# Hybrid layer step: convolution rows asked for by GpSimd, cache pages by SyncE, and one set of query weights for the last two routings

## The reference, cut to what matters

```python
xn = rmsnorm(hp, norm1[l])
qa, ka, va, qkv_b, z, b_raw, a_raw = project(xn, w_in[l], q_norm[l], k_norm[l])
oa = diff_attn_prompt(qa, ka, va, lam, slopes)               # group A, 4 heads
gq, gk, gv, gg, gbeta, conv_new = gdn_inputs(qkv_b, ...)      # group B: 4-tap convolution, silu
ob, s_new = gdn_prompt(gq, gk, gv, gg, gbeta)
hp = hp + merge_heads(oa, ob, z, ..., w_out[l], hp.dtype)     # mixer projection
hp = hp + peer_ffn(rmsnorm(hp, norm2[l]), peer_wq[l], peer_keys[l], peer_u[l], peer_v[l])
# the sample tokens do the same; their keys and values of the past come from paged caches:
kpast = cache_k[l][page_table]        # 8 sequences x 8 pages of 128 positions
vpast = cache_v[l][page_table]
```

## Time and profile before

| | us |
|---|---|
| median of 3 runs | 2095.93 |
| lowest, highest | 2095.76, 2103.09 |
| the profiled execution | 2104.38 |
| its span in the trace | 2102.70 |

### The profile page before, as it was taken

The page is one execution under the profiler, slowest core; times in us unless marked ns, Lnnn a source line. Parts: engine busy times, 40 slices in busy tenths (PEclk is TensorE's granted clock), DMA queues, the critical chain, the costliest instruction groups (busy, mean ns, idle before and its releaser), DMA issues.

```text
span 2102.7 us, 20559 instructions
## 1 busy us (share of the span) xinstructions
PE 1716.8 (82%) x6211; PEld 863.4 (41%) x6211; DVE 1333.7 (63%) x3023; ACT 801.2 (38%) x2371; POOL 788.4 (37%) x704
## 2 busy tenths in 40 slices
PE   5888899988897878989787888979696566876777
PEld 1333354647453435445344444534452222542111
DVE  1344524344796666987666788766588865679554
ACT  1342322231643632564543346363244332333433
POOL 3123010111344443435345343534443554455442
PEclk9889899999998999999899999999898897998999
DMA  9999543127899999999999999999999999999997
GB/s 337 322 345 349 198 138 102 58 101 308 354 426 369 427 427 428 426 426 414 428 415 427 427 426 408 414 426 417 426 426 412 427 427 428 427 427 427 427 427 315
DMA packets 137192, 774.90 MB, mean 369 GB/s; under 512 B 14832, under 2 KB 23808, under 8 KB 59753
## 3 DMA queue, kind: packets, MB, share of 16 engines
q0 software_dynamic: 88384, 621.30, 70.8%
q1 hardware_dynamic: 45216, 144.98, 18.6%
q10 hardware_dynamic: 3480, 7.31, 0.9%
HBM read 757.55 MB, written 16.26 MB: 368 GB/s over the span
## 4 chain that ended last, share of the span: by engine, by line
DMA 34%; PE 33%; DVE 17%; ACT 7%; issue 4%; POOL 2%; SPq 1%; POOLq 1%; ACTq 0%; another core or an unknown queue 0%; DVEq 0%
DMA sb_uv<-in_peer_uv,sb_eidx 29%; PE bank L2180 15%; DVE sb_uv L1768 7%; PE bank L1789 6%; PE bank L2109 2%; PE bank L2147 2%; DVE sb_hres L1742 2%; DMA sb_hres<-pre_conv 1%; POOL sb_uv L973 1%; ACT sb_diag L1347 1%; ACT L1336 1%; ACT sb_ew L1340 1%; PE bank L1903 1%; PE bank L1915 1%; DMA sb_xin<-pre_conv 1%
## 5 line engine op out<-in xcount | busy, mean ns | idle before, releaser
L2180 PE MATMUL bank<-sb_uv,sb_diag 128*128 128x512 f32 (+1 forms) x1860 | 961.0, 653 | 299.9 <-ACT sb_diag L1347 289.6
L973 POOL DMA_INDIRECT sb_uv<-in_peer_uv,sb_eidx x576 | 694.5, 1206 | 886.4 <-PE bank L2180 680.1
L1768 DVE CUSTOM_DVE_ANT_0 sb_uv<-sb_uv,sb_xn 128x1024 f32<-128x1024 f32 x576 | 699.4, 1221 | 313.8 <-DMA sb_uv<-in_peer_uv,sb_eidx 311.0
L2180 PEld LDWEIGHTS bank<-sb_uv,sb_diag 128*128 128x128 f32 (+1 forms) x1860 | 337.8, 197 | 798.7 <-ACT sb_diag L1347 471.9
L1336 ACT ACTIVATE sb_gel<-sb_h 128x1 f32<-128x1 f32 x576 | 116.3, 202 | 791.7 <-DVE sb_h L1768 785.4
L1789 PE MATMUL bank<-sb_w,sb_xnT 128*128 128x512 f32 (+1 forms) x560 | 271.6, 627 | 38.0 <-DMA sb_w<-in_w_sections 25.1
L1347 ACT ACTIVATE sb_diag<-sb_stay,sb_ew 128x128 f32<-128x128 f32 (+1 forms) x465 | 183.2, 394 | 47.5 <-PE bank L2180 4.6
L1340 ACT ACTIVATE sb_ew<-sb_gel,sb_gate 128x1 f32<-128x1 f32 x576 | 169.7, 295 | 19.8
L1789 PEld LDWEIGHTS bank<-sb_w,sb_xnT 128*128 128x128 f32 (+1 forms) x560 | 100.0, 190 | 164.1 <-issue 120.3
L2147 PEld LDWEIGHTS bank<-sb_rT,sb_zone 128*128 128x128 f32 x1216 | 146.7, 194 | 25.4 <-issue 25.4
L2147 PE MATMUL bank<-sb_rT,sb_zone 128*128 128x128 f32 x1216 | 148.0, 277 | 1.8 <-issue 1.8
(11 more groups left out here) (338 smaller groups left out, 1550.7 us busy)
## 6 DMA issues: line engine op xcount, KB each, us to landing
sb_zone<-in_w_route SPq DMA_DIRECT2D x17, 2304.0 KB
sb_w<-in_w_sections SPq DMA_DIRECT2D x40, 512.0 KB, 8.6
sb_zone<-in_w_mixer SPq DMA_DIRECT2D x8, 2048.0 KB
sb_uv<-in_peer_uv,sb_eidx POOLq DMA_INDIRECT x576
sb_attended<-in_cache_v POOLq DMA_DIRECT2D x32, 256.0 KB, 6.6
sb_sS<-in_cache_kT SPq DMA_DIRECT2D x32, 256.0 KB, 4.4
sb_zone<-in_cache_v POOLq DMA_DIRECT2D x32, 256.0 KB, 6.6
sb_zone<-in_cache_kT SPq DMA_DIRECT2D x32, 256.0 KB, 3.9
```

Source lines behind the costliest of these rows:

```text
L973: nc.gpsimd.indirect_dma_start(uv[:, m % RING, :], None, i["peer_uv"], bass.IndirectOffsetOnAxis(ap=eidx[:, t % 2, n:n + 1], axis=0)).then ...
L1768: nc.vector.tensor_tensor_reduce(out=uv[:, m % RING, 0:D], in0=uv[:, m % RING, 0:D], in1=xn2[:, t % 2, :], scale=1.0, scalar=0.0, op0=ALU. ...
L2180: ins = nc.tensor.matmul(bank[half][0:rows, :], lhsT=G["diag"][:, d % DIAGS, 0:rows], rhs=uv[:, m % RING, D + 512 * half:D + 512 * half + ...
```

## The change

1. **Queues.** `conv_inputs` (convolution rows and tap weights) moves from SyncE to GpSimd, its waits with it. `value_loads` moves from GpSimd to SyncE. Due times: the halves of the first pair's keys from 38.5 and 39.5 to 41 and 45, of its values from 42 and 51 to 50.5 and 55.5; later pairs' second value half one unit later. The first key store (`k_store`, unit 1) goes from 4 to 15 after its unit.
2. **Places.** `attended`, `pot`, `kqv`, `zg`, `vmeta`, `qS` and `qt` become one tensor `held`. Pieces 0 and 1 of tile 3 (parts 2, 3) go into it, over state, vectors, keys, values and queries; pieces 2 and 3 into `zone`. The sample tile uses all four where they are, in the order g = 0 to 3, and `turn_of` goes.
3. **Waits of tile 3's loads.** Parts 2 and 3 wait for the end of the prompt's attention and the last use of the recurrent vectors instead of for the mixer halves; parts 4 and 5 for the mixer halves instead of for scores. They are due at steps -1, 2, 8, 11 instead of 4, 7, 24, 32.
4. **Sample mixer weights** come in four quarters of 1 MB into `mix_part`, which lies over attention's scores and weights; each waits for the use of the quarter before (`s_mxw`, `s_yp`). The sample mixing starts 10 slots earlier, its later steps 4 slots earlier.

```diff
-    return SLOTS * (n - 1) + (74 + 1.05 * k if n < PT else 46 + 1.05 * k + (8 if k >= 4.9 else 0))
+    return SLOTS * (n - 1) + (74 + 1.05 * k if n < PT else 36 + 1.05 * k + (14 if k >= 4.9 else 0))
+def last_mix_at(c):
+    return route_at(PT, 2) + 5 * c
...
+        sizes = (HW, 2 * HW, 3 * HW, HW, NH * TOK, NT * HW, HW, NH * NSAMP, NH * 128)
+        held = keep("held", [128, sum(sizes)])
+        edges = [sum(sizes[:n]) for n in range(len(sizes) + 1)]
+        obl, _, kqv, zg, kT, vtok, vmeta, qS, qt = (held[:, a:b] for a, b in zip(edges, edges[1:]))
...
+        G["S"] = G["Sw"][:, 0:4 * NPOS].rearrange("p (a n) -> p a n", a=2)
+        G["wT"] = G["Sw"][:, 4 * NPOS:].rearrange("p (a n) -> p a n", a=2)
+        mix_part = G["Sw"][:, 2 * NPOS:2 * NPOS + 4 * HW]
...
-            if n == PT and part in (0, 1, 2):
-                return attended[:, 0:ZONE]
-            return R["zone"][:, part % 2 if n < PT or part > 3 else 0, :]
+            if n >= PT - 1 and part in (2, 3):
+                first = edges[1] + ZONE * (part - 2)
+                return held[:, first:first + ZONE]
+            return R["zone"][:, part % 2, :]
...
-                    yield after(QK_UNIT[u], 4)
+                    yield after(QK_UNIT[u], 4 if u else 15)
...
                 def route_loads(n):
+                    apart = n + 1 == PT
                     for part in range(6):
-                        yield route_at(n, (-18, -17, 4, 7, 24, 32)[part])
+                        yield route_at(n, (-18, -17, -1, 2, 8, 11)[part] if apart else (-18, -17, 4, 7, 24, 32)[part])
...
+                        elif apart and part < 4:
+                            sp.wait_ge(s_pv, NH * PT)
+                            sp.wait_ge(s_vst, 16 * (NT + 1))
+                            sp.wait_ge(s_vec, 3 * NT)
+                            sp.wait_ge(s_DT, 2 * NT)
+                            sp.wait_ge(s_tr, 4 * NT)
+                            sp.wait_ge(s_wr[part % 2], 16 * (3 * n + 1))
+                        elif apart:
+                            sp.wait_ge(s_yp, 2 * n + part - 3)
+                            sp.wait_ge(s_wr[part % 2], 16 * (3 * n + 2))
...
-                def last_route_loads():
+                def last_mixer_loads():
+                    for c in range(4):
+                        yield last_mix_at(c) - (8 if c == 0 else 4)
+                        if c == 0:
+                            sp.wait_ge(s_pv, NH * PT)
+                        elif c % 2:
+                            sp.wait_ge(s_mxw, c // 2 + 1)
+                        else:
+                            sp.wait_ge(s_yp, 2 * PT + 1)
+                        cols = slice(4 * HW * (c % 2), 4 * HW * (c % 2) + 4 * HW)
+                        sp.dma_start(mix_part, i["w_mixer"][c // 2][:, cols]).then_inc(s_wrl, 16)
...
-                        yield past_at(p - 1, 5 + 2 * half) if p else early_at(38.5 + half)
+                        yield past_at(p - 1, 5 + 2 * half) if p else early_at(41 + 4 * half)
...
+                def value_loads(p):
+                    for half in range(2):
+                        yield past_at(p - 1, 27 + 2 * half) if p else early_at(50.5 + 5 * half)
...
+                            if p:
+                                sp.wait_ge(s_dpv, p)
+                            for g in range(4):
+                                sp.dma_start(cache_quarter(k)[:, g, :], i["cache_v"][bass.ds(pages[g], 1)].rearrange("g p n -> (g p) n")).then_inc(s_vals, 16)
...
+                def conv_inputs():
+                    for m in range(3 * NT):
...
+                        yield conv_at(m) - 9
+                        if n == 0:
+                            if m:
+                                pool.wait_ge(s_conv, 3 * (m - 1) + 1)
+                            pool.dma_start(cw, i["conv_w"][0:1, :, ch].broadcast_to([128, CONV_W, HW])).then_inc(s_cw, 16)
+                        yield conv_at(m) - 8
...
+                        pool.wait_ge(s_raw[m % 2], 16 * raw_count(m))
...
+                            pool.dma_start(cv[b][:, :, :], taps(META + 128 * t, 128, ch)).then_inc(s_cv[b], 16)
...
-                    j = turn_of(n, g)
+                    j = g
...
+                            yield route_at(n, 2 + 3 * half + 1.5 * part) if n < PT else last_mix_at(2 * half + part)
+                            if n == PT:
+                                pe.wait_ge(s_wrl, 16 * (2 * half + part + 1))
```

More of the change, by code:

```diff
@@ L2100, in mix @@
                         for part in range(2):
-                            yield route_at(n, 2 + 3 * half + 1.5 * part)
+                            yield route_at(n, 2 + 3 * half + 1.5 * part) if n < PT else last_mix_at(2 * half + part)
+                            if n == PT:
+                                pe.wait_ge(s_wrl, 16 * (2 * half + part + 1))
+                            elif part == 0:
+                                pe.wait_ge(s_wr[half], 16 * (3 * n + 1))
                             if part == 0:
-                                if n < PT:
-                                    pe.wait_ge(s_wr[half], 16 * (3 * n + 1))
-                                else:
-                                    pe.wait_ge(s_wrl, 16 * (half + 1))
                                 pe.wait_ge(s_mxc, 2 * (n + 1))
-                            for k in range(4 * part, 4 * part + 4):
-                                ins = nc.tensor.matmul(bank[6 + half][:, :], lhsT=R["rT"][:, k, :], rhs=weights_part(n, half)[:, k, :], start=k == 0, stop=k == KC - 1)
+                            weights = weights_part(n, half)[:, 4 * part:4 * part + 4, :] if n < PT else mix_part.rearrange("p (k n) -> p k n", k=4)
+                            for k in range(4):
+                                ins = nc.tensor.matmul(bank[6 + half][:, :], lhsT=R["rT"][:, 4 * part + k, :], rhs=weights[:, k, :], start=part + k == 0, stop=part == 1 and k == 3)
+                            if n == PT and part == 0:
+                                ins.then_inc(s_mxw, 1)
                         ins.then_inc(s_yp, 1)
```

118 lines of the change are left out of this document (40 added, 78 removed).

## The result

| | before | after |
|---|---|---|
| median of 4 runs each | 2095.85 | 2074.75 |
| lowest, highest | 2095.22, 2103.09 | 2070.40, 2077.05 |
| the profiled execution, its span | 2104.38, 2102.70 | 2075.32, 2073.50 |
| first gather in the trace | 504.75 | 493.34 |
| bytes moved | 774.90 MB | 770.18 MB |

The ratio is 0.9884, with a 95% interval of 0.9857 to 0.9911 (some 2066 to 2077 us). The forecast was 2075.

The account below looks back on a forecast made before the run. DMA was taken to bound the kernel from 575 us on, a chain of waits across queues the front. -10 and -11 make -21, from the median 2095.93 to 2075 us; range 2060 to 2092.

Parts of the forecast that it names:

- Part 1: Last routing: query weights stay in place, 4.72 MB fewer bytes at 427 GB/s; -10 us, bounds -12 to -7.
- rival 2: Choice of experts: VectorE takes over and half of the query weights' saving is lost; 2080 us, chance 0.13.
- One cover: Sample tile's mixer: 1 MB loads asked for 11 us before use land in about 5.5 us, so they are hidden.
- Part 2: Front: queues exchanged between SyncE and GpSimd; steps sum to -10.8, taken as -11 us, bounds +6 and -20.
- Step a: Front, 31 to 99 us: weight piece 15 and first rows come earlier, tables become next late; -3.7 us.
- Step b: Front, 99 to 189 us: GpSimd's root no longer behind value pages, TensorE's weight-piece and fold waits shrink; -2.8 us.
- Step c: Front, 189 to 240 us: four weight pieces ahead of the last values, rows on their own queue; -6.3 us.
- Step d: Front, 240 to 262 us: unit 13's rows stand behind the sample output's root on GpSimd; +2 us.
- The ceiling: Front: 225 us at DMA share 0.94 are 211 us of full DMA, so 14 us at most unless loads move later.
- rival 1: Front gives nothing, tables and rows as late with DMA at share 0.94; only -10 us counts, 2086 us, chance 0.22.
- Rival 3: Front: SyncE becomes the bound, keys come late and three pairs grow by 7 us each; 2107 us, chance 0.07.
- The other mark: First gather to the end: about 1588 us instead of 1598, at 427 GB/s, with 16 query weight loads.

Follow-up runs that it names:

- E2: The changed kernel with the queue exchange and new due times undone, so only the weight places and loads change; ratio to the kernel before 0.9940.
- E4: The kernel before, unchanged, run once more for a second trace; first gather 505.34 us, stage behind it 1592.3 us.
- E1: The kernel before with only the queues exchanged and the due times changed, no new weight places; ratio 0.9948.
- E3: The changed kernel with 4.46 MB of mixer weights loaded again, which nothing reads or waits for; ratio to the kernel before 0.9957.
- E5: The kernel before with convolution rows and tap weights moved to GpSimd, value pages staying there at old due times; ratio 1.0069.
- E9: The changed kernel with value pages of pairs 1 to 3 loaded at half width, 6.29 MB left out; ratio to the kernel before 0.9904.
- E7: The changed kernel with small column weights and first gate tables loaded ahead of pair 0's value pages; ratio to the kernel before 0.9887.
- E8: The changed kernel with tables first and weight pieces 22 to 25 asked for ahead of pair 3's keys; ratio to the kernel before 0.9879.
- E11: The changed kernel with the key and value page due times of the kernel before; ratio to the kernel before 0.9934.

## Why the prediction was right, step by step

**Part 1: -10 expected, -11.1 measured, give or take 4** (the two groups of stages; 11.05 by bytes). No loss at VectorE shows, though 1600 to 1625 has it busy 24.83 of 25: the DMA share stayed 1.01 there, and rival 2's loss of 5 us did not come. The query weight pieces 0 and 1 of tile 3 came 13 and 16 slots earlier (counted from the first gather) and not 5, which cost nothing either. One cover did not hold, that of the 1 MB mixer quarters:

```profile
1681.77 28.70 SPq L794 DMA_DIRECT2D sb_Sw<-in_w_mixer  x3
```

```profile
1675.51 6.22 PE L2125 MATMUL bank<-sb_Sw,sb_rT 128*128 128x512 f32 x8 [0.73 <-ACT sb_rT L1287]
1690.56 5.40 PE L2125 MATMUL bank<-sb_Sw,sb_rT 128*128 128x512 f32 x8 [3.67 <-DMA sb_Sw<-in_w_mixer]
```

The prediction had them asked for 11 us ahead and landing in 5.5. But all quarters go to one place, so a quarter can go out only when the one before is used: at 1681.77, while TensorE came for it 5.1 us later, and it took 8.8 to land. TensorE waited 3.67, 3.55 and 3.07 us at 1690.56, 1704.91 and 1719.13. No loss of that kind shows in the length of the stage, as the step said for the case without cover (the eight gather buffers would absorb it).

**Part 2: -11 expected; the first gather moved by -11.41**, and by the sample block of three old fronts (mean 260.1) and three new ones (mean 248.8) -11.3. The sum is right. Its terms are not, and that they cancel is luck. One pair of traces is too few to tell the terms, since the same front differs by 3 us and more from one execution to the next. The start of each pair's value products, and the sample block:

| | pair 0 | pair 1 | pair 2 | pair 3 | sample block |
|---|---|---|---|---|---|
| before | 99.16 | 144.02 | 184.61 | 235.56 | 261.71 |
| E2 | 98.91 | 144.79 | 187.30 | 232.46 | 258.16 |
| E4 | 99.43 | 146.92 | 188.99 | 234.75 | 260.41 |
| after | 102.59 | 137.14 | 178.16 | 223.44 | 250.33 |
| E1 | 99.97 | 136.62 | 175.48 | 220.64 | 247.66 |
| E3 | 100.53 | 135.50 | 175.76 | 221.43 | 248.34 |
| new less old, means | +1.9 | -8.8 | -10.5 | -12.4 | -11.3 |

- *Step a (-3.7, bounds +4 and -8): wrong in sign, +1.9* (+3.4 in the pair before and after). Piece 15 went out by 31.4 us and the 14.44 us went, as said; the first rows reached VectorE at 61.78 (said 61). The tables were issued at 75.90 (said 74.5) but landed nearly as slowly as before, after 12.6 us (said 9). The small columns came at 88.56 instead of 83. The term that was mis-sized is the landing. (The step doesn't show how it comes to -3.7: 83 for 86.06 would be -3.)
- *Step b (-2.8, bounds 0 and -8.9): far too small, -12.4, past its bound.* The waits of 2.22 and 5.53 shrank to 0 and 2.13 (the fold's was 9.50 and 5.59 in E2 and E4, 2.63 and 2.54 in E1 and E3), and the fold went from 3.67 to 2.00 us, a gain of the clock that the step did not count. E5 shows how much hangs on the roots, which the step priced at part of its -1.6; VectorE's waits for them fell from 19.5 to 8.1 us over the front. How the -12.4 splits further is not shown.
- *Step c (-6.3): too large, -1.9* (-5.7 in the pair before and after). The weight piece's wait did not vanish but grew from 4.41 to 8.96: its four pieces went ahead of the last values, as said, but behind 32 other pages. The fold's wait fell by 6.2 instead of 2.6, and its matmuls by 1.67, where the step said that nothing comes back.
- *Step d (+2): right in kind, +1.1 in size.* The root ran at 238.25 and unit 13's rows went out right behind it, at 240.14; the wait at the sample block grew from 1.65 to 3.13. The four steps make 1.9 - 12.4 - 1.9 + 1.1 = -11.3.
- *Landings and issues.* Rows from GpSimd cost 0.75 to 0.83 us (said 1) and landed after 7.9 and 8.7 us (said 8 to 10).

**The ceiling was no ceiling.** The prediction limited the front's gain by the DMA share (225 us at 0.94 are 211 of full DMA). E9 speaks against it: with 6.29 MB less the share falls and the time hardly. The same holds for the argument given for rival 1. The Trainium skill (DMA: Bandwidth & Descriptors, Issuing engines are not separate DMA queues) says that another issuer saves only the time to initiate, usually small beside the transfer. Here the issue is not small: 8 pages with their lookups hold the engine for some 9 us, while their 2.1 MB are 6.3 us at the front's 335 GB/s. Where they stand decides between 1.0069 (E5) and 0.9948 (E1).

**What bounds the new front is open.** Rival 3 said that it would be SyncE. A pair takes SyncE 38.8 to 39.4 us now (112.63, 151.38, 190.74), 37 were said, and it has no slack between 110 and 205. E7 and E9 fit that, since there the pieces behind the pages are what TensorE waits for longest; E8 does not: there SyncE lost 8 us, pair 3's last values went out 5.3 us later than in E7 (204.22 against 198.95), and its value products began at the same time (221.47 against 221.56). The chain of that stretch also runs through rows, convolution and the writing back of rows, and TensorE is busy most of it. No kernel here gave SyncE less to issue at the same order; moving one half of the value pages to an engine with free time was not tried.

**The first gather as a mark.** "What the front gains arrives at the first gather undiminished" held for the change (-11.38 at the sample block, -11.41 at the gather). It did not hold for E9, whose 5 us were lost again behind that mark, for a reason that lies not in its edit (the last section). The other mark, 1588 us from there to the end, was reckoned from a long execution: the traces give 1580.2, and a mean of 1582.1 for all that keep the weights.

## What to carry to other kernels

Ask of each queue not how busy it is but what stands behind its long groups: two moves that each cost time alone (here 0.7%, and 0.2% at the edge of what the runs can tell) can gain 0.5% together, since each clears the place that the other needs, and the due times have to be set anew with them (E11). A DMA share above 0.9 is no proof that bytes bound a stretch; leave some bytes out and see whether the time follows. It did in the gather stage (E2, E3, share 1.00), and hardly in the front (E9). Before bringing a load forward, look at what holds it: an engine that no longer waits for anything pushes another load back (E7), and a buffer that isn't free stops the queue (E8). And take the terms of a sum from several executions of each kernel.
